# Two layer boundaries by halves of 128 tokens: a transformer forward pass on one Trainium2 core

## The chip, the cores and the metric

One NeuronCore of a Trainium2 chip. The metric is device microseconds of one execution on that core. The kernel is written engine by engine, with its semaphores set by hand: TensorE (PE in the profile) multiplies, VectorE (DVE) and ScalarE (ACT) do the elementwise work, GpSimd (POOL) helps, and SyncE (SP) issues the weight loads.

## The reference, cut to what matters

256 tokens with 2048 features go through two layers of the first block (gated attention of three kinds, then an output matrix and a LayerNorm), then through a second block. All is fp32. What the change touches:

```python
def hybrid_layer(x, mem, w_in, b_forget, w_mem_kv, w_out, ln_gain, ln_bias):
    h = jnp.einsum('bsd,dn->bsn', x, w_in)
    ...
    y = jnp.concatenate([y_fox, y_dsa, y_mem], axis=-1)
    y = jnp.einsum('bsn,nd->bsd', y, w_out)
    return layer_norm(ALPHA * x + y, ln_gain, ln_bias)
```

The LayerNorm is over the 2048 features of one token: rows do not depend on each other, but each needs the whole row of `y @ w_out`. What follows at both boundaries is a product with the normalised rows: layer 1's `w_in` after layer 0, the second block's `w_in` after layer 1.

## The kernel before, in words

**Blocks and the ring.** Every weight matrix is read in blocks of 128x1024 elements (512 KB). `plan` (line 94) lists the blocks in the order in which they are used; a chunk is the set of blocks that sum into one pair of accumulators `acc`, one accumulator bank for each half of 128 tokens (`s` = 0, 1). SP loads a block into a ring of four (`raw`, `RING` = 4). ScalarE rounds it to `high` (`round_block`, line 858), and VectorE forms what is left, `low = raw - high` (`low_part`, line 475). In some stretches, listed in `pool_blocks` (line 462), GpSimd does this instead: every second block from 40 to 133 of a layer and blocks 18 to 83 of the second block. The activations have a high and a low part as well (`xh`, `xl` for the features, `yh`, `yl` for the attention's output). TensorE forms high x high, high x low and low x high (`weight_block`, line 617). The high part of block g may be written only when TensorE has used block g - 4 (`block_used`), and `raw` only when its low part is formed.

**Chunks of w_out.** `COLS` (line 76) cuts the 2048 columns in three chunks of 512 and two of 256. In a chunk of 512 a block holds two row tiles of 512 columns, in one of 256 four row tiles of 256. A wide block is 2 row tiles x 2 token halves x 3 = 12 products of 512 columns; a narrow one 24 of 256. Both chunks of 256 together are the last eight blocks of a layer.

**The order of the work.** Each engine has its own program. Within a layer (162 blocks) VectorE and ScalarE keep ahead of TensorE through `slots` (line 400), and do side work between blocks. At the end of a layer `last_sides` (line 411) closes the list. Behind it, at the boundary:
- VectorE (lines 1465 to 1499) adds the residual of the last chunk when its last block is done (`add_residual`, line 1358), takes the statistics in pieces of 256 columns (line 1364), aggregates them per row (line 1470) and forms the variance.
- ScalarE takes the root (line 956); VectorE forms scale and shift of the rows in five small steps (lines 1233 to 1236, 1475).
- ScalarE normalises `x` in units of 256 columns, for both halves of the tokens (`normalise`, line 1044).
- TensorE, which has meanwhile run 36 filler products (`spin`, line 757, whose results nobody reads), transposes a unit into one of two banks `tb` (four 128x128 transposes, line 587).
- VectorE applies gain and bias out of the bank (`affine`, line 1478, products at line 1488), ScalarE rounds (`affine_high`, line 1051), VectorE forms the low part (line 1497).
- TensorE takes up the first block of the next product as soon as unit 0 is there. Block u needs unit u, since a block covers 256 features; the remaining six units are transposed between the blocks.

The order in time is what is written: an instruction that waits holds all behind it on its engine. The low parts of the first three blocks behind the boundary are formed by VectorE before the wait for the last product (`last_sides` with `LEAD - 1`; the third one behind it in the loop), and ScalarE rounds the first three in its `last_sides`.

**GpSimd** loads the rows of gain and bias at the boundary, when the last w_out block is used (lines 1734 and 1735); they are first needed by `residual` (line 1337), at block 18 of layer 1, or at block 3 of the second block, some 30 us after the boundary.

## Time and profile before

| what | value |
| --- | --- |
| median of 3 runs | 2205.16 us (2201.83 to 2205.2) |
| the profiled execution | 2201.67 us |
| its span, first to last instruction | 2199.9 us |
| mean granted clock of TensorE | 0.996 of full speed |

The profile describes one execution. Times in it are microseconds from its first instruction. A duration of an instruction includes its way through the engine, so that two in a row overlap by some 0.1 us in it. A row of the instructions in order of time ends, in brackets, with the idle time before it and what ended that. "issue" is time in which the engine waited for nothing that the profile shows. L662 is line 662 of the kernel.

### The profile page before, as it was taken

To read this page: it belongs to the slowest core of one execution; us is meant where nothing else is said; L and a number is where in the kernel's file an instruction comes from. 1 tells how busy PE (TensorE), PEld (TensorE's weight loads), DVE (VectorE), ACT (ScalarE), POOL (GpSimd) and SP (SyncE) were. 2 spreads that over 40 slices of the span, in tenths; PEclk is the share of its full clock that TensorE was granted. 3 is DMA by queue.
4 is the path that set the end of the run, shared out by engine and by line. 5 is a ranking of instruction groups with operands and counts; after the bars stand their busy time and mean duration, and the time that the engine had idled before them with its cause. 6 is when DMAs were issued, how large, how long until landed. Compare 5 with 4: busy or idle time off the path is not lost.

```text
span 2199.9 us, 29501 instructions
## 1 busy us (share of the span) xinstructions
PE 2157.8 (98%) x11798; PEld 1864.2 (85%) x11798; DVE 1278.4 (58%) x1851; ACT 1101.3 (50%) x1525; POOL 401.4 (18%) x176
## 2 busy tenths in 40 slices
PE   8999999999999999999999999999999999999997
PEld 7888888888988888888888888788888888888886
DVE  5544448765566337855577666665555555555555
ACT  4444554554354554555455455646535534544543
POOL 0000333431000334332006876000000000000000
PEclk9999999999999999999999999999999999999998
DMA  8666555655666555565656655545666666666663
GB/s 279 194 182 186 157 149 158 177 163 173 191 177 190 163 153 153 169 176 163 188 168 200 191 174 161 191 145 170 192 192 192 190 192 192 189 192 193 190 192 126
DMA packets 324313, 394.66 MB, mean 179 GB/s; under 512 B 20257, under 2 KB 252321, under 8 KB 323409
## 3 DMA queue, kind: packets, MB, share of 16 engines
q1 hardware_dynamic: 322528, 383.20, 57.9%
q0 software_dynamic: 1648, 9.58, 1.2%
q8 instruction: 94, 1.54, 0.3%
q14 instruction: 43, 0.34, 0.0%
HBM read 390.63 MB, written 2.10 MB: 179 GB/s over the span
## 4 chain that ended last, share of the span: by engine, by line
PE 90%; DVE 4%; ACT 3%; issue 2%; DMA 1%; SPq 0%; DVEq 0%; ACTq 0%
PE acc L645 32%; PE acc L660 16%; PE acc L662 12%; PE acc L647 12%; PE acc L648 12%; ACT high L863 1%; PE tb L708 1%; PE tb L587 1%; ACT sc L895 1%; PE obank L730 1%; DVE low L477 1%; PE sbank L754 1%; ACT sc L906 0%; PE sbank L698 0%; DVE yf L1225 0%
## 5 line engine op out<-in xcount | busy, mean ns | idle before, releaser
L863 ACT ACTIVATE high<-raw 128x1024 fp32r<-128x1024 f32 (+1 forms) x729 | 764.4, 1051 | 789.8 <-PE acc L660 197.9
L477 DVE TENSOR_TENSOR low<-raw,high 128x1024 fp32r<-128x1024 f32 (+1 forms) x569 | 710.6, 1250 | 632.6 <-ACT high L863 629.5
L645 PE MATMUL acc<-xhl,high 128*128 128x512 f32 x3200 | 778.7, 393 | 4.1 <-ACT cb L1152 2.2
L645 PEld LDWEIGHTS acc<-xhl,high 128*128 128x128 f32 x3200 | 585.8, 189 | 117.2 <-issue 2.8
L477 POOL TENSOR_TENSOR low<-raw,high 128x1024 fp32r<-128x1024 f32 x160 | 393.8, 2465 | 744.2 <-ACT high L863 744.0
L660 PE MATMUL acc<-xhl,low 128*128 128x256 f32 x3200 | 432.3, 285 | 2.7 <-DVE low L477 1.4
L660 PEld LDWEIGHTS acc<-xhl,low 128*128 128x128 f32 x3200 | 416.1, 191 | 20.9 <-DVE xhl L1643 1.7
L647 PE MATMUL acc<-high,yhl 128*128 128x512 f32 (+1 forms) x1044 | 383.8, 374 | 1.4 <-DVE work L1517 1.4
L648 PE MATMUL acc<-high,yhl 128*128 128x512 f32 (+1 forms) x1044 | 382.0, 372 | 0.0
L662 PE MATMUL acc<-low,yhl 128*128 128x512 f32 (+1 forms) x1044 | 242.9, 373 | 0.5 <-DVE yhl L1619 0.2
L647 PEld LDWEIGHTS acc<-high,yhl 128*128 128x128 f32 x1044 | 196.7, 188 | 36.1 <-DVE work L1517 1.8
L648 PEld LDWEIGHTS acc<-high,yhl 128*128 128x128 f32 x1044 | 196.7, 188 | 34.0
L662 PEld LDWEIGHTS acc<-low,yhl 128*128 128x128 f32 x1044 | 184.8, 188 | 35.7 <-DVE yhl L1619 1.1
L647 PE MATMUL acc<-high,xhl 128*128 128x512 f32 (+1 forms) x320 | 108.1, 353 | 1.0 <-issue 1.0
L1200 DVE TENSOR_TENSOR acc<-acc,cross 128x512 f32<-128x512 f32 x104 | 72.3, 695 | 61.8 <-ACT cross L883 61.6
L648 PE MATMUL acc<-high,xhl 128*128 128x512 f32 (+1 forms) x320 | 106.5, 349 | 0.0
L1553 DVE SCALAR_TENSOR_TENSOR tb<-work,params,tb 128x256 f32<-128x256 f32 x232 | 93.6, 481 | 0.0
L895 ACT ACTIVATE sc<-sc,small 128x128 f32<-128x128 f32 x64 | 28.6, 448 | 107.5 <-DVE small L1276 107.5
L662 PE MATMUL acc<-low,xhl 128*128 128x512 f32 (+1 forms) x320 | 69.8, 354 | 0.0
L647 PEld LDWEIGHTS acc<-high,xhl 128*128 128x128 f32 x320 | 61.0, 190 | 10.0 <-issue 2.2
L648 PEld LDWEIGHTS acc<-high,xhl 128*128 128x128 f32 x320 | 61.0, 191 | 7.5
L883 ACT ACTIVATE cross<-acc 128x512 f32<-128x512 f32 x104 | 60.4, 580 | 0.0
(199 smaller groups left out, 1268.2 us busy)
## 6 DMA issues: line engine op xcount, KB each, us to landing
raw<-in_w_in SPq DMA_DIRECT2D x336, 512.0 KB, 3.7
raw<-in_w_ff SPq DMA_DIRECT2D x256, 512.0 KB, 4.4
raw<-in_w_out SPq DMA_DIRECT2D x91, 512.0 KB, 4.5
raw<-in_w_mem_kv SPq DMA_DIRECT2D x32, 512.0 KB, 4.7
raw<-in_w_out SPq DMA_DIRECT2D x10, 256.0 KB, 2.7
x_nat<-in_mem SPq DMA_DIRECT2D x4, 512.0 KB, 7.6
x_nat<-in_x POOLq DMA_DIRECT2D x4, 512.0 KB, 5.7
yf<-in_ln_gain POOLq DMA_DIRECT2D x2, 1024.0 KB, 5.2
```

The lines of the kernel that those rows point to most:

```text
L477: eng.tensor_tensor(part(low, g), part(raw, g), part(high, g).bitcast(F32), ALU.subtract).then_inc(ready, 1)
L587: ins = pe.transpose(t[:, dt * S + s * P:dt * S + s * P + P], src[:, s, first + dt * P:first + dt * P + P], ident)
L645: ins = pe.matmul(acc[:, 2 * (c.acc % 2) + s, :], wh[:, t, at], vhl, start=first, stop=last)
L647: pe.matmul(outs[s], vh[:, at], wh[:, t, :], start=first, stop=False)
L648: ins = pe.matmul(outs[s], vl[:, at], wh[:, t, :], start=False, stop=last)
L660: ins = pe.matmul(acc[:, 2 * (c.acc % 2) + s, S:2 * S], wl[:, t, at], vh, start=False, stop=last)
L662: ins = pe.matmul(outs[s], vh[:, at], wl[:, t, :], start=False, stop=last)
L863: act.activation(part(high, g), part(raw, g), ACT.Copy).then_inc(high_ready, 1)
L883: act.activation(cross, crosses(c), ACT.Copy).then_inc(cross_ready, 1)
L895: ins = act.activation(sc[:, j % 2, s, 0:n], src, ACT.Exp, bias=nmx[:, r:r + 1], accum_out=rs[:, r:r + 1])
L1200: dve.tensor_tensor(accs(c), accs(c), cross, ALU.add).then_inc(folded, 1)
L1553: ins = dve.scalar_tensor_tensor(out=cv[:, ct, :] if tap == TAPS - 1 else sums_at, in0=src, scalar=w, in1=sums_at, op0=ALU.mult, op1=ALU.add)
```

## The change

The output matrix is cut in four chunks of 512 columns (`FCOLS`) instead of five. The last four blocks of w_out (`out`) and the first four behind the boundary (`into`) are passed twice, first for tokens 0 to 127, then for tokens 128 to 255; all four stay in the ring meanwhile. `weight_block` takes the halves as `rows`; `block_used` rises at the second pass, and the new semaphore `rows_half` when the last of `out` has been passed for the first half. TensorE's order is written out in `edge`, and the filler is gone. Residual, statistics, variance, root, scale and the first four units of normalising, transposing, gain and bias, rounding and low part are done per half. The statistics are taken over 512 columns at once, everywhere. The low parts of the first three blocks of `into` go to GpSimd, ahead of its loads of the rows; ScalarE rounds these blocks only behind the first root. The counters of the semaphores follow. The filler before the feed-forward stage stays.

```diff
-        for n, (col, width) in enumerate(COLS):
+        for n, (col, width) in enumerate(FCOLS):
...
-        def norms(phase, u):
-            return 5 * phase + (u + 1 if u < 2 else 2 + u // 2)
+        def norms(phase, u, s=0):
+            if phase < DEPTH:
+                return 8 * phase + (3 * s + min(u, 2) + 1 if u < 4 else 7 + (u - 4) // 2)
+            return 8 * DEPTH + (u + 1 if u < 2 else 2 + u // 2)
+        def tiles_in(phase, u, s=0):
+            return 12 * phase + (4 * s + u + 1 if u < 4 else 8 + u - 3)
+        edges = [(by[("o", l, NF - 1)].blocks[-4:], by[("fv", l + 1, 0) if l + 1 < DEPTH else ("v2", 0)].blocks[:4])
+                 for l in range(DEPTH)]
...
-        pool_blocks = [[LAYER0 + LAYER_SLOTS * l + b for b in range(40, 134) if b % 2] for l in range(DEPTH)]
+        pool_blocks = [[LAYER0 + LAYER_SLOTS * l + b for b in range(40, 134) if b % 2] + edges[l][1][:3]
+                       for l in range(DEPTH)]
...
-            def weight_block(g):
+            def weight_block(g, rows=(0, 1)):
...
-                tiles = [(t, c.kt0 + c.nk * i + t, s) for t in range(c.nk) for s in range(len(outs))]
+                tiles = [(t, c.kt0 + c.nk * i + t, s) for t in range(c.nk) for s in rows[:len(outs)]]
...
-                ins.then_inc(block_used, 1)
+                if 1 in rows:
+                    ins.then_inc(block_used, 1)
+                elif g == c.blocks[-1]:
+                    ins.then_inc(rows_half, 1)
...
+            def half_transposes(l, s, u):
+                pe.wait_ge(norm_ready, norms(l, u, s))
+                t = t_begin(("nT", l, u, s))
+                for dt in range(2):
+                    ins = pe.transpose(t[:, dt * S + s * P:dt * S + s * P + P],
+                                       x[:, s, 256 * u + dt * P:256 * u + dt * P + P], ident)
+                t_end(ins, ("nT", l, u, s))
+            def full_transposes(l, u):
+                pe.wait_ge(norm_ready, norms(l, u))
+                transpose_unit(("nT", l, u), x, 256 * u)
+            def edge(l):
+                out, into = edges[l]
+                for g in out:
+                    weight_block(g, (0,))
+                for g in out[:3]:
+                    weight_block(g, (1,))
+                half_transposes(l, 0, 0)
+                weight_block(out[3], (1,))
+                half_transposes(l, 0, 1)
+                half_transposes(l, 0, 2)
+                weight_block(into[0], (0,))
+                half_transposes(l, 0, 3)
+                weight_block(into[1], (0,))
+                weight_block(into[2], (0,))
+                half_transposes(l, 1, 0)
+                weight_block(into[3], (0,))
+                half_transposes(l, 1, 1)
+                half_transposes(l, 1, 2)
+                weight_block(into[0], (1,))
+                half_transposes(l, 1, 3)
+                weight_block(into[1], (1,))
+                full_transposes(l, 4)
+                weight_block(into[2], (1,))
+                full_transposes(l, 5)
+                weight_block(into[3], (1,))
+                for u in range(4, 8):
+                    if u < 6:
+                        full_transposes(l, u + 2)
+                    weight_block(into[3] + u - 3)
...
-                spin(job_no(l, "dsa", HS - 1), 36)
-                for u in range(2):
-                    pe.wait_ge(norm_ready, norms(l, u))
-                    transpose_unit(("nT", l, u), x, 256 * u)
+                edge(l)
...
-                last_sides(round_block, layer_side, g0, LAYER_SLOTS)
+                last_sides(round_block, layer_side, g0, LAYER_SLOTS, 0)
                 nxt = g0 + LAYER_SLOTS
-                root(l + 1)
+                root_half(0)
+                round_block(nxt)
+                act.wait_ge(nmr_ready, 2 * l + 1)
+                normalise(0, 1, (0,))
+                normalise(1, 1, (0,))
+                round_block(nxt + 1)
+                affine_high(0, 0)
+                normalise(2, 2, (0,))
+                affine_high(1, 0)
+                round_block(nxt + 2)
+                affine_high(2, 0)
+                root_half(1)
+                affine_high(3, 0)
                 round_block(nxt + 3)
-                act.wait_ge(nmr_ready, l + 1)
-                normalise(0)
-                normalise(1)
-                normalise(2, 2)
-                for u in range(8):
-                    affine_high(8 * l + u)
-                    if u in (0, 2):
-                        normalise(u + 4, 2)
-                    if u >= 2:
-                        round_block(nxt + 2 + u)
+                act.wait_ge(nmr_ready, 2 * l + 2)
+                normalise(0, 1, (1,))
+                normalise(1, 1, (1,))
+                affine_high(0, 1)
+                normalise(2, 2, (1,))
+                affine_high(1, 1)
+                normalise(4, 2, (0, 1))
+                affine_high(2, 1)
+                affine_high(3, 1)
+                round_block(nxt + 4)
+                normalise(6, 2, (0, 1))
+                round_block(nxt + 5)
+                for u in range(4, 8):
+                    affine_high(u)
+                    round_block(nxt + 2 + u)
...
+                def row_stats(n, s):
+                    last[0] = step(dve.bn_stats(stats[:, s, n, :], x[:, s, CW * n:CW * n + CW]))
...
+                def last_residual(s, l=l):
+                    n = NF - 1
+                    c = by[("o", l, n)]
+                    at = x[:, s, CW * n:CW * n + CW]
+                    if s:
+                        acc_done(c)
+                    else:
+                        dve.wait_ge(rows_half, l + 1)
+                    ins = dve.scalar_tensor_tensor(out=at, in0=at, scalar=ALPHA, in1=accs(c)[:, s, :], op0=ALU.mult,
+                                                   op1=ALU.add)
+                    if s:
+                        ins.then_inc(sum_ready, 1)
+                        dve.wait_ge(sum_ready, sums("o", l, n))
+                    else:
+                        link(ins)
+                def row_var(s):
+                    dve.wait_ge(dve_done, last[0])
+                    link(dve.bn_aggr(mv[:, s, :], stats[:, s, :, :].rearrange("p c k -> p (c k)")))
+                    dve.tensor_scalar(var[:, s:s + 1], mv[:, s, 1:2], LN_EPS, None, ALU.add).then_inc(var_ready, 1)
+                def row_scale(s, l=l):
+                    at = slice(s, s + 1)
+                    dve.wait_ge(std_ready, 2 * l + s + 1)
+                    link(newton(var[:, at], std[:, at], rstd[:, at], nt[:, at]))
+                    dve.scalar_tensor_tensor(out=nmr[:, at], in0=mv[:, s, 0:1], scalar=-1.0, in1=rstd[:, at], op0=ALU.mult,
+                                             op1=ALU.mult).then_inc(nmr_ready, 1)
...
-                last_sides(low_block, layer_side, g0, LAYER_SLOTS, LEAD - 1)
-                nxt = g0 + LAYER_SLOTS
-                add_residual(NC - 1)
-                dve.wait_ge(dve_done, last[0])
-                for s in range(ST):
-                    step(dve.bn_aggr(mv[:, s, :], stats[:, s, :, :].rearrange("p c k -> p (c k)")))
-                dve.wait_ge(dve_done, n_done[0])
-                dve.tensor_scalar(var, mv[:, :, 1], LN_EPS, None, ALU.add).then_inc(var_ready, 1)
-                dve.wait_ge(std_ready, l + 1)
-                link(newton(var, std, rstd, nt))
-                dve.scalar_tensor_tensor(out=nmr, in0=mv[:, :, 0], scalar=-1.0, in1=rstd, op0=ALU.mult,
-                                         op1=ALU.mult).then_inc(nmr_ready, 1)
-                def affine(n):
...
+                def affine(u, s=0, l=l):
+                    t = t_wait(dve, ("nT", l, u, s) if u < 4 else ("nT", l, u))
...
+                    for dt in range(2):
+                        kt = 2 * u + dt
+                        at = slice(dt * S + s * P, dt * S + s * P + P) if u < 4 else slice(dt * S, dt * S + S)
+                        ins = dve.tensor_scalar(cb[:, u % 4, at], t[:, at], g[:, kt:kt + 1], b_[:, kt:kt + 1],
+                                                ALU.mult, ALU.add)
+                    ins.then_inc(aff_ready, 1)
+                def affine_low(u, s=0, l=l):
+                    at = slice(s * P, s * P + P) if u < 4 else slice(0, S)
+                    dve.wait_ge(hi_ready, 16 + tiles_in(l, u, s))
+                    dve.tensor_tensor(xl[:, 2 * u:2 * u + 2, at], pair(cb[:, u % 4, :])[:, :, at],
+                                      xh[:, 2 * u:2 * u + 2, at].bitcast(F32), ALU.subtract).then_inc(xt_ready, 1)
+                last_sides(low_block, layer_side, g0, LAYER_SLOTS, 0)
+                nxt = g0 + LAYER_SLOTS
+                last_residual(0)
+                row_stats(NF - 1, 0)
+                row_var(0)
+                row_scale(0)
+                affine(0, 0)
+                affine_low(0, 0)
+                affine(1, 0)
+                last_residual(1)
+                affine_low(1, 0)
+                affine(2, 0)
+                row_stats(NF - 1, 1)
+                affine_low(2, 0)
+                affine(3, 0)
+                row_var(1)
+                affine_low(3, 0)
+                row_scale(1)
+                low_block(nxt + 3)
+                affine(0, 1)
+                affine(1, 1)
+                affine_low(0, 1)
+                affine(2, 1)
+                affine_low(1, 1)
+                affine(3, 1)
+                affine_low(2, 1)
+                affine_low(3, 1)
+                low_block(nxt + 4)
+                affine(4)
+                low_block(nxt + 5)
+                for u in range(4, 8):
                     if u < 7:
-                        affine(8 * l + u + 1)
-                    dve.wait_ge(hi_ready, 16 + 8 * l + u + 1)
-                    dve.tensor_tensor(xl[:, 2 * u:2 * u + 2, :], pair(cb[:, u % 4, :]),
-                                      xh[:, 2 * u:2 * u + 2, :].bitcast(F32), ALU.subtract).then_inc(xt_ready, 1)
+                        affine(u + 1)
+                    affine_low(u)
                     low_block(nxt + 2 + u)
```

## Rows read from the trace of the kernel before

**Rows 1.** The page, busy time: us (share of the span) xinstructions.

```profile
PE 2157.8 (98%) x11798; PEld 1864.2 (85%) x11798; DVE 1278.4 (58%) x1851; ACT 1101.3 (50%) x1525; POOL 401.4 (18%) x176
```

**Rows 2.** The chain of waits, 592 to 640 us: start, us, what.

```profile
594.79 1.92 PE acc L662 x16
...
616.91 0.44 PE tb L587 x4
...
634.73 1.81 PE acc L662 x8
```

**Rows 3.** Instructions of TensorE in order of time, both boundaries: start, us, line, shapes.

```profile
604.23 4.48 PE L761 MATMUL sbank<-xhl 128*128 128x256 f32 x36
...
612.83 0.76 PE L647 MATMUL acc<-high,xhl 128*128 128x512 f32 x1 [0.32 <-issue]
...
638.20 0.28 PE L641 MATMUL sbank<-xhl,high 128*86 128x256 f32 x1
...
1114.17 4.48 PE L761 MATMUL sbank<-xhl 128*128 128x256 f32 x36
...
1122.77 0.47 PE L647 MATMUL acc<-high,xhl 128*128 128x512 f32 x1 [0.64 <-issue]
...
1147.04 1.98 PE L645 MATMUL acc<-xhl,high 128*128 128x512 f32 x8
```

**Rows 4.** The chain of waits at the first boundary: start, us, what.

```profile
604.43 0.70 DVE x_nat L1358
605.15 0.76 DVE small L1364 x2
605.94 0.61 DVE small L1470 x2
...
606.78 0.21 ACT small L956
...
608.00 3.50 ACT x_nat L1048 x6
```

**Rows 5.** Groups by line and shape: xcount, busy us, mean ns, idle before.

```profile
L863 ACT ACTIVATE high<-raw 128x1024 fp32r<-128x1024 f32 x715 | 755.1, 1058 | 774.2 <-PE acc L660 197.9 <-PE acc L645 188.5 <-PE acc L662 184.7
...
L477 POOL TENSOR_TENSOR low<-raw,high 128x1024 fp32r<-128x1024 f32 x160 | 393.8, 2465 | 744.2 <-ACT high L863 744.0
...
L926 ACT ACTIVATE yhl<-y 128x256 fp32r<-128x256 f32 x32 | 13.2, 413 | 0.4 <-DVE y L1295 0.4
...
L1364 DVE BATCH_NORM_STATS2 small<-x_nat 128x6 f32<-128x256 f32 x32 | 11.4, 415 | 0.3
...
L1497 DVE TENSOR_TENSOR xhl<-cb,xhl 128x512 fp32r<-128x512 f32 x16 | 11.0, 684 | 0.4 <-ACT xhl L1054 0.4
...
L1048 ACT ACTIVATE x_nat<-x_nat,small 128x512 f32<-128x512 f32 x12 | 9.0, 801 | 0.0
...
L1488 DVE TENSOR_SCALAR cb<-tb,params 128x256 f32<-128x256 f32 x16 | 8.0, 540 | 4.7 <-PE tb L587 4.7
...
L1254 DVE SCALAR_TENSOR_TENSOR yf<-tb,small,consts 128x128 f32<-128x128 f32 x12 | 4.2, 352 | 34.8 <-PE tb L689 34.8
```

**Rows 6.** One line of VectorE: xcount, min/median/max ns, first and last start us.

```profile
L1301 DVE TENSOR_TENSOR yhl<-y,yhl x32: 399/420/2605, 240.2 to 1044.3; 128x256 fp32r<-128x256 f32 x32
```

**Rows 7.** Instructions of GpSimd and VectorE in order of time, 486 to 492 and 871 to 877 us.

```profile
487.21 2.39 POOL L477 TENSOR_TENSOR low<-raw,high 128x1024 fp32r<-128x1024 f32 x1 [4.50 <-ACT high L863]
487.29 2.58 DVE L1301 TENSOR_TENSOR yhl<-y,yhl 128x256 fp32r<-128x256 f32 x1
...
871.47 2.41 POOL L477 TENSOR_TENSOR low<-raw,high 128x1024 fp32r<-128x1024 f32 x1 [2.15 <-ACT high L863]
872.65 0.69 DVE L1222 TENSOR_TENSOR cb<-acc,consts 128x512 f32<-128x512 f32 x1
```

**Rows 8.** Busy time by stretch: us, PE, PEld, DVE, ACT, POOL busy (x), granted clock, DMA share, GB/s.

```profile
610.00:615.00 5.00, 3.80 (x13) 2.81 (x14) 4.78 (x9) 4.13 (x8) 0.00 (x0) 0.67 0.32 124
...
1120.00:1125.00 5.00, 3.54 (x18) 2.72 (x19) 4.78 (x9) 4.13 (x8) 0.00 (x0) 1.00 0.36 125
```

101 lines of the change are left out of this document (46 added, 55 removed).

## The prediction

> **What bounds the kernel now.** I read the page first, then the order of time on TensorE around each layer boundary, then the chain of waits there. TensorE is busy for 98% of the span [rows 1], so only what TensorE computes, or where it computes nothing, can move the time. A product with 512 columns takes 0.227 us at the full clock, one with 256 takes 0.12 [rows 2]. A block of the narrow kind (24 products of 256) therefore takes 2.88 us, a wide one (12 of 512) 2.72, and a unit of four transposes 0.44 [rows 2].
>
> At the boundary between the layers the last product of w_out ends at 604.23, the next layer's first starts at 612.83, and its eighth block is done at 638.20; at the second boundary these are 1114.17, 1122.77 and 1147.04 [rows 3]. Between, TensorE runs filler products and three transpose units. Count each boundary from the first of the last eight w_out blocks (8 x 2.88 = 23.04 before 604.23) to the end of the eighth block behind it: 638.20 - 581.19 = **57.0 us**, and 1147.04 - 1091.13 = **55.9 us**. The work in it is 23.04 + 8 x 2.72 + 8 x 0.44 = 48.3, so 8.7 and 7.6 us are stalls, 16.3 together. The chain shows what fills them: the residual (0.70), the statistics (0.76 and 0.61), root and scale, and six normalising steps in a row (3.50) [rows 4]. The filler costs nothing now and its removal gives nothing.
>
> The first boundary is 1.1 us longer than the second, with the same steps: there the granted clock is 0.67 in the 5 us around the return of the products, at the second 1.00 [rows 8]. TensorE had run filler and then only transposes before it fell.
>
> **The change, part by part.**
>
> *Wide last blocks.* The eight w_out blocks of columns 1536 to 2047 become wide: 8 x 0.16 = 1.3 us less per boundary, on TensorE's path and hidden by nothing. The residual in mid-way falls away beside other work. I take **-2.6 us** for both; this is the surest term.
>
> *The new order.* The last four w_out blocks pass for rows 0 to 127, then for rows 128 to 255, and the norm of the first half runs under the second pass. Half a block is 6 x 0.227 = 1.36 us. The number of products and of transposes stays the same, so the work from the first of these four blocks to the eighth behind is 12 x 2.72 + 8 x 0.44 = 36.2 us. The question is how much stall is left. VectorE must do more: each affine unit of the first four is cut in two pieces. I take for the new shapes:
> - affine on 128 columns out of PSUM: 0.41 us, between 0.35 (a row of that shape, another operation) and 0.54 (256 columns) [rows 5]. Issued behind one another each costs 0.09 less. A unit thus costs 2 x 0.64 = 1.3 instead of 0.9.
> - statistics over 512 columns: 0.67, from 0.41 for 256 [rows 5] plus 256 elements more, which cost 0.26 on VectorE between 420 ns [rows 6] and 684 [rows 5]. Bounds 0.41 and 0.82.
> - ScalarE's rounding of half a unit: 0.41 [rows 5], bounds 0.35 and 0.63; normalising 0.80 for 512 columns [rows 5] and 0.5 in a row for 256, as now (six steps of both kinds take 3.50, [rows 4]). The low parts of the activations by halves: 0.42 [rows 6], bounds 0.35 and 0.68.
> - The low parts of the next three weight blocks move to GpSimd: 2.40 us each where nothing holds it up (mean 2.47, [rows 5]), instead of 1.2 on VectorE.
>
> That last move has a price that the list of durations hides. While GpSimd forms a low part (487.21, 2.39 us), a VectorE subtraction of 128x256 with both inputs in SBUF takes 2.58 us instead of the median 0.42 [rows 6]; it ends just after GpSimd does. One with an input in PSUM runs at its usual 0.69 in the middle of such a step [rows 7]. So the affine steps and the residual (PSUM) run on, but the low parts of the activations (both inputs in SBUF) wait for GpSimd. The Trainium skill (SBUF — State Buffer, SBUF: two separate sides) says that a VectorE instruction with two SBUF inputs and a GpSimd one hold a shared port pair exclusively, and whoever starts first blocks the other for the whole instruction. By that rule the sum is the one below; without it, it would be the first rival's.
>
> Now laid out by hand, each engine in its written order, 0.03 us from an engine to the next (0.1 to a product), time 0 at the first of the last four blocks:
> - 5.44: first half passed. Residual, statistics, aggregate, variance to 7.55; root 7.58 and five small steps to 8.73, 1.2 in all as now (606.78 to 608.00, [rows 4]); ScalarE, having rounded weight block 0 from 7.69 to 8.74 (1.06, [rows 5]), normalises units 0 and 1 by 9.84. TensorE is still in the second pass: the transposes of unit 0 start at 9.52 with **no stall**, where 8.6 us lie between the products now. This is what the change wins.
> - GpSimd's low part of block 0 runs 8.82 to 11.22, just when VectorE wants its first subtraction, at 11.15. VectorE gets in at 11.22; GpSimd's next runs 11.56 to 13.96, the third 14.30 to 16.70. VectorE's second and third subtractions wait for the ends of these, at 13.96 and 16.70.
> - Stalls of TensorE: **0.5** (unit 2 normalised), **0.8** (low part of unit 1), **1.4** (of unit 2).
> - VectorE reaches the second half's variance only at 18.0 and its scale at 20.0, since it also has the third and fourth affine units of the first half. TensorE has finished block 2 at 18.6 and waits for the second half's first transposes until 20.7: **2.1**. Then 0.3 for the low part of block 3, which stands behind the scale on VectorE, 0.2 and **0.9** for the first subtraction of half two.
> - From there no stall until block 4: VectorE has the low part of block 4, affine unit 4, the low part of block 5 and affine unit 5 (1.2 + 0.9 + 1.2 + 0.9, and half a microsecond of waits, from 28.1) in front of unit 4's subtraction, done at 33.2; TensorE is ready at 31.2: **2.1**. After it the old rhythm holds.
>
> Sum of stalls 8.4 per boundary, 44.6 us to the end of the eighth block. With the four wide blocks ahead (10.9): 55.5 for each boundary. Before: 57.0 and 55.9. **Sum: 2 x 55.5 - 112.9 = -1.9 us**; in words, -2.6 by wide blocks, and stalls of 16.9 for 16.3, cut small but not shortened. The falling clock of the first boundary is in the 57.0 and taken as gone.
>
> *Edits at nothing:* the LayerNorm row loads leave GpSimd's queue only behind its third low part (16.7), some 6 us behind the last w_out block instead of at once, and are needed 30 us after the boundary; that slack is their cover, and without it VectorE's later residual would wait. SP's queue has each weight load behind the low part four blocks earlier: block 4's load can start after 11.2 and is wanted at 27, some 16 us for a load, while the steady rhythm has one land every 2.7. Counters and names cost nothing.
>
> The profiled execution took 2201.67 us (span 2199.9); the median of the three runs is 2205.16, 3.5 above it. -1.9 from the median gives **2203.3**. A measurement of this kernel can tell about 0.2%, 4.4 us, from no change.
>
> **The rivals.**
> - *The port does not bind*, because GpSimd's steps miss VectorE's. The same layout without it has stalls of 0.6, 0.2, 1.6, 0.3, 0.2, 0.9 and 2.1, so 42.2 instead of 44.6: 53.1 per boundary, -6.7 us: **2198.5**. For it: VectorE works much on PSUM. Against: the steps that ended with GpSimd's [rows 7], and the two want the port in the same 0.1 us.
> - *GpSimd wins the first race.* VectorE asks at 11.15 and GpSimd is free at 11.22; 0.1 us more in the rounding of the half unit, and GpSimd's second low part goes first, until 13.6. Then block 0 itself waits 1.9 and the third block 2.0: 46.6, or 57.5 per boundary, +2.1: **2207.3**. If the half affine costs 0.54, or the rounding 0.63, the same branch comes out, with some 47.5 at the most, +3.9.
> - *The clock falls in the new gaps*, the slower one. Twice per boundary TensorE has only transposes and waits for over 2.5 us (18.6 to 21.3, and 30.8 to 33.3). A fall costs 1.1 (57.0 against 55.9) to 1.7 us (a granted clock of 0.67 over 5 us, [rows 8]). Four falls: -1.9 + 4.4 to 6.8, up to **2210.1**. It decides from four falls at 1.6 each on. For it: the clock fell once in two such gaps. Against: those gaps held 4 us without a full stretch of products, the new ones less. The Trainium skill (TensorE: Matmul & The Clock Gate, HAM oscillation) says that short groups of products between waits throttle again and again; that speaks against this change, and by it the time is this rival's.
> - *The change does not act*, since the second pass still waits for all rows: the semaphore for the first half is raised by the last of the four first-half passes, so no; in the rest.
>
> **How the numbers follow.** Forecast 0.37 (no change), port free 0.22 (faster), GpSimd first 0.24 (no change), clock 0.11 (slower), rest 0.06, half to each side. So faster 0.25, within 0.2% 0.61, slower 0.14. The range takes in the first rival with half a microsecond below it, and the second with its dearest shapes (+3.9, 2209.1): 2198.0 to 2209.3.
>
> **What would show it.** In the profile after: no filler, and transposes starting at once behind the third second-half block (right or wrong for the overlap); VectorE subtractions of 128x256 with 1.2 us or more beside GpSimd steps (the port); TensorE idle before the second half's first transposes and before the fifth block, 2 us each; granted clock 1.00 at both boundaries. TensorE idle below 6 us per boundary would show the layout too dear, one product group at half clock the third rival.

## The result, and the profile after

The changed kernel takes 2207.82 us (median of 13 runs, 2206.4 to 2210.43) where the kernel before takes 2203.35 (13 runs, 2200.14 to 2206.61): a ratio of 1.0021, with a 95% interval of 1.0013 to 1.0030. The forecast was 2203.3, a shade below the kernel before; the time came out 4.5 us above it, inside the range that was given and on its slow side. The forecast had started from 2205.16, the median of three runs, which lies 1.8 above the median of thirteen: as a change, -1.9 was forecast and +4.5 came, which is a miss of 6.4. The profiled execution has a span of 2204.6, against 2199.9.

Busy time on the page of the changed kernel; TensorE's is 7.6 us less than before [rows 1], though two fillers of 4.48 us are gone [rows 3], so what it computes takes no less time than it did, and the longer span is more idle time:

```profile
PE 2150.2 (98%) x11534; PEld 1845.8 (84%) x11534; DVE 1283.1 (58%) x1865; ACT 1101.5 (50%) x1535; POOL 415.7 (19%) x182
```

Instructions of TensorE in order of time at the first boundary and, behind the second line of dots, at the second: start, us, line, shapes, and in brackets the idle time ahead and what ended it. The last row of each group is the first product behind the eighth block. They answer to [rows 3].

```profile
600.83 0.38 PE L775 MATMUL tb<-consts,x_nat 128*128 128x128 f32 x2
...
603.19 0.44 PE L775 MATMUL tb<-consts,x_nat 128*128 128x128 f32 x2 [0.38 <-ACT x_nat L1098]
605.20 0.47 PE L657 MATMUL acc<-high,xhl 128*128 128x512 f32 x1 [1.57 <-issue]
...
609.93 0.50 PE L657 MATMUL acc<-high,xhl 128*128 128x512 f32 x1 [1.43 <-DVE xhl L1586]
...
613.42 0.44 PE L775 MATMUL tb<-consts,x_nat 128*128 128x128 f32 x2 [1.85 <-ACT x_nat L1098]
...
617.07 0.47 PE L657 MATMUL acc<-high,xhl 128*128 128x512 f32 x1 [0.79 <-issue]
...
626.25 0.50 PE L657 MATMUL acc<-high,xhl 128*128 128x512 f32 x1 [1.86 <-DVE xhl L1586]
...
639.34 0.28 PE L651 MATMUL sbank<-xhl,high 128*86 128x256 f32 x1
...
1112.72 0.38 PE L775 MATMUL tb<-consts,x_nat 128*128 128x128 f32 x2
...
1151.21 1.07 PE L655 MATMUL acc<-xhl,high 128*128 128x512 f32 x4
```

The filler is gone, the first transposes of the half (600.83) stand among the products of w_out, and the products that take the new operand begin at 605.20, 7.6 us earlier than before (612.83). So the overlap that the change is written for is there. But TensorE is stopped seven times behind the first half transposes, 8.0 us in all (six of the seven are shown; the seventh is 0.15 at 614.02). From the first half transposes to the end of the eighth block it takes 38.5 us at each boundary; the first of the last eight w_out blocks starts 20.4 us ahead of them, in this kernel and in every one below that has its TensorE order. That makes **58.9 us for both boundaries**, where the kernel before has 57.0 and 55.9: +1.9 and +3.0, together 4.9, and the spans differ by 4.7. The rest of the kernel is the same within 0.8 us.

Two causes are to be seen. The first is in GpSimd's and VectorE's instructions in order of time, first and second boundary. The row in the second place shows the second of the two low parts of the row ahead of it by itself:

```profile
600.10 4.72 POOL L487 TENSOR_TENSOR low<-raw,high 128x1024 fp32r<-128x1024 f32 x2 [83.88 <-ACT high L913]
602.47 2.35 POOL L487 TENSOR_TENSOR low<-raw,high 128x1024 fp32r<-128x1024 f32 x1
602.47 2.63 DVE L1586 TENSOR_TENSOR xhl<-cb,xhl 128x256 fp32r<-128x256 f32 x1 [0.49 <-ACT xhl L1108]
...
607.96 1.92 DVE L1586 TENSOR_TENSOR xhl<-cb,xhl 128x256 fp32r<-128x256 f32 x1
...
1112.00 4.72 POOL L487 TENSOR_TENSOR low<-raw,high 128x1024 fp32r<-128x1024 f32 x2 [83.88 <-ACT high L913]
1114.37 2.63 DVE L1586 TENSOR_TENSOR xhl<-cb,xhl 128x256 fp32r<-128x256 f32 x1 [0.49 <-ACT xhl L1108]
```

GpSimd runs its first two low parts one behind the other. The rows of the second low part and of VectorE's first subtraction both start at 602.47, a tie to the hundredth of a microsecond. The low part takes its usual 2.35 and the subtraction 2.63 instead of 0.42: it ends 0.28 behind the second low part (605.10 and 604.82), so GpSimd had the port. Block 0 waits for it (605.20). The row calls that wait "issue"; who is late is read from VectorE's row.

The second cause is the clock. Busy time by stretch (the columns are those of [rows 8]; the third figure from the right is the granted clock), and one product of that stretch:

```profile
625.00:630.00 5.00, 3.75 (x10) 3.00 (x11) 4.97 (x8) 2.21 (x3) 0.00 (x0) 0.71 0.83 155
...
1140.00:1145.00 5.00, 5.00 (x20) 3.94 (x19) 3.63 (x7) 2.32 (x3) 0.00 (x0) 0.75 0.69 210
```

```profile
627.46 0.63 PE L657 MATMUL acc<-high,xhl 128*128 128x512 f32 x1
```

A product of 512 columns takes 0.23 us from the start of one to that of the next; from 627.05 to 629.16 the starts are 0.42 apart, the 1.2 GHz level in place of 2.4. Ahead of it TensorE had waited 1.86 us before the fifth block; the clock was still high for the first 0.8 us of products behind that wait (626.25 to 627.05). This happens once per boundary, behind the same wait, where before it happened at the first boundary only.

### The profile page after: what moved, and what is told of

Same layout as the page of the kernel before. It is cut to its first block, busy times and chain, and to the rows that moved or that the text cites. A ratio compares the mean times of both kernels' runs of the same rounds, so it can differ in the third digit from the quotient of the medians.

```text
span 2204.6 us, 29019 instructions
## 1 busy us (share of the span) xinstructions
PE 2150.2 (98%) x11534; PEld 1845.8 (84%) x11534; DVE 1283.1 (58%) x1865; ACT 1101.5 (50%) x1535; POOL 415.7 (19%) x182
## 3 DMA queue, kind: packets, MB, share of 16 engines
q1 hardware_dynamic: 318432, 383.20, 57.8%
## 4 chain that ended last, share of the span: by engine, by line
PE 89%; DVE 6%; ACT 3%; issue 2%; DMA 1%; SPq 0%; DVEq 0%; ACTq 0%
PE acc L655 32%; PE acc L670 16%; PE acc L672 12%; PE acc L657 12%; PE acc L658 12%; ACT high L913 1%; PE tb L721 1%; DVE low L487 1%; ACT sc L945 1%; PE obank L743 1%; DVE xhl L1586 1%; PE sbank L767 1%; ACT sc L956 0%; PE tb L597 0%; PE sbank L711 0%
## 5 line engine op out<-in xcount | busy, mean ns | idle before, releaser
L487 DVE TENSOR_TENSOR low<-raw,high 128x1024 fp32r<-128x1024 f32 (+2 forms) x563 | 703.1, 1250 | 630.3 <-ACT high L913 627.3
L487 POOL TENSOR_TENSOR low<-raw,high 128x1024 fp32r<-128x1024 f32 x166 | 408.2, 2463 | 910.2 <-ACT high L913 910.0
L657 PE MATMUL acc<-high,yhl 128*128 128x512 f32 (+1 forms) x980 | 377.6, 387 | 1.4 <-DVE work L1641 1.4
L658 PE MATMUL acc<-high,yhl 128*128 128x512 f32 (+1 forms) x980 | 375.8, 385 | 0.0
L657 PEld LDWEIGHTS acc<-high,yhl 128*128 128x128 f32 x980 | 184.2, 188 | 38.5 <-DVE work L1641 1.8
L658 PEld LDWEIGHTS acc<-high,yhl 128*128 128x128 f32 x980 | 184.1, 188 | 36.4
L672 PEld LDWEIGHTS acc<-low,xhl 128*128 128x128 f32 x320 | 52.7, 193 | 9.5 <-issue 2.1
```

The costliest lines, as they stand in the source:

```text
L487: eng.tensor_tensor(part(low, g), part(raw, g), part(high, g).bitcast(F32), ALU.subtract).then_inc(ready, 1)
L657: pe.matmul(outs[s], vh[:, at], wh[:, t, :], start=first, stop=False)
L658: ins = pe.matmul(outs[s], vl[:, at], wh[:, t, :], start=False, stop=last)
L672: ins = pe.matmul(outs[s], vh[:, at], wl[:, t, :], start=False, stop=last)
```

## Experiments

"Boundaries" are counted as above, from the first of the last eight w_out blocks to the end of the eighth block behind, in the profiled execution. "Ratio" is to runs of the kernel before on the same chip, with its 95% interval; the median of before there stands beside it.

| kernel | median us (n) | before | ratio | boundaries us |
|---|---|---|---|---|
| changed | 2207.82 (13) | 2203.35 | 1.0021 [1.0013, 1.0030] | 58.9, 58.9 |
| e1 wide blocks alone | 2204.18 (11) | 2202.31 | 1.0007 [0.9998, 1.0016] | 56.8, 57.9 |
| e2 GpSimd's low parts short | 2201.39 (11) | 2202.31 | 0.9992 [0.9983, 1.0001] | 56.5, 55.2 |
| e3 GpSimd waits | 2201.95 (11) | 2202.31 | 0.9995 [0.9986, 1.0004] | 57.8, 57.2 |
| e4 fillers | 2203.69 (11) | 2202.31 | 1.0002 [0.9994, 1.0011] | 55.4, 55.4 |
| e6 e3 and e4 | 2201.38 (11) | 2201.94 | 0.9997 [0.9988, 1.0006] | 55.6, 55.7 |
| e11 VectorE late, fillers | 2205.25 (11) | 2203.34 | 1.0007 [0.9998, 1.0016] | 57.3, 57.3 |
| e12 VectorE late | 2208.32 (11) | 2203.34 | 1.0023 [1.0014, 1.0032] | 58.9, 58.9 |
| e9 two lines exchanged | 2205.11 (11) | 2202.69 | 1.0010 [1.0001, 1.0020] | 56.1, 56.1 |
| e5 reordered | 2197.65 (11) | 2201.94 | 0.9977 [0.9968, 0.9986] | 52.6, 52.6 |
| e7 reordered, two low parts | 2197.85 (8) | 2201.94 | 0.9976 [0.9966, 0.9987] | 52.8, 52.8 |
| e8 reordered, GpSimd waits | 2194.61 (5) | 2201.94 | 0.9964 [0.9952, 0.9977] | 50.9, 50.9 |
| e10 reordered, exchanged | 2196.06 (5) | 2202.69 | 0.9961 [0.9949, 0.9974] | 51.4, 51.3 |

### e1: the wide blocks alone

The kernel before, with w_out in four chunks of 512 columns.

```
-        for n, (col, width) in enumerate(COLS):
+        for n, (col, width) in enumerate(FCOLS):
             c = chunk(("o", l, n), a["w_out"][l], col, width=width)
...
-                add_residual(NC - 1)
+                add_residual(NF - 1)
```

> The kernel before with the output matrix cut in four chunks of 512 columns and nothing else of the change. By the sum of the prediction this alone is worth 8 x 0.16 us per boundary: 2.6 us less than the kernel before, a ratio of 0.9988, with the boundary itself (filler, three units of transposes, first product 8.6 us after the last) as it was. If instead the narrow blocks cost nothing on TensorE's path, the ratio is 1.000. If the slowing of the changed kernel came from the wide cut, this kernel is slower than before.

No gain: 1.0007, with an interval that leaves out the 2.6 us (0.9988). In order of time, TensorE, VectorE, and TensorE again:

```profile
602.59 4.47 PE L761 MATMUL sbank<-xhl 128*128 128x256 f32 x36
...
602.79 1.22 DVE L1358 SCALAR_TENSOR_TENSOR x_nat<-x_nat,acc 128x1024 f32<-128x1024 f32 x1 [3.06 <-PE acc L648]
604.05 1.41 DVE L1364 BATCH_NORM_STATS2 small<-x_nat 128x6 f32<-128x256 f32 x4
...
612.38 0.77 PE L647 MATMUL acc<-high,xhl 128*128 128x512 f32 x1 [0.18 <-issue]
```

The products end at 602.59 instead of 604.23, 1.6 us earlier: 1.3 by the eight wide blocks, and 0.4 because the first of them starts earlier (580.83 for 581.19). But the last chunk is now 512 columns for the norm's chain too: the residual takes 1.22 for 0.70 and the statistics 1.41 for 0.76 [rows 4]. The first product is 0.45 us earlier, at 612.38. The first boundary, with one fall of the clock before and here, is 0.2 us shorter (56.8 for 57.0). The second is 2.0 longer (57.9 for 55.9): there the clock falls here (0.50 at 1120 to 1125) and did not before. In front of a serial chain, a wider last chunk moves work from TensorE to the chain.

### e2: GpSimd's part of the port taken away

```
                 for g in pool_blocks[l]:
+                    if g in edges[l][1]:
+                        pool.wait_ge(high_ready, g + 1)
+                        n = slice(0, 32)
+                        pool.tensor_tensor(part(low, g)[:, :, n], part(raw, g)[:, :, n], ...)
+                        continue
                     low_part(pool, g, low_pool)
```

It leaves out 480 of 512 columns of three low parts per boundary.

> The changed kernel, with GpSimd's three low parts at each boundary formed for 32 of 512 columns only (the rest of these low parts is left out), so that GpSimd holds the shared port for a moment instead of 2.4 us each. All waits and orders stay. Port theory: no VectorE subtraction of 128x256 takes over 0.5 us, the stalls before blocks 0 and 2 of the new product go, and the eight blocks of w_out to the eighth behind the boundary take 53.1 to 53.3 us instead of 58.9, up to 9 us less in all than the changed kernel, ratio to the kernel before 0.997. Rival (the halves themselves cost it, VectorE's doubled instructions): under 2 us less than the changed kernel.

GpSimd now takes 0.32 us a block, and no subtraction of VectorE is above 0.43. TensorE's first product with the new operand is at 603.87, right behind the transposes:

```profile
600.59 0.32 POOL L1858 TENSOR_TENSOR low<-raw,high 128x64 fp32r<-128x64 f32 x1 [83.84 <-ACT high L913]
...
603.87 0.48 PE L657 MATMUL acc<-high,xhl 128*128 128x512 f32 x1
```

Counted from the first half transposes, that product comes after 2.56 us instead of 4.37, and the waits of 1.57 before block 0 and 1.43 before block 2 are gone. The ratio falls by 0.0029, 6.4 us. The rival, that the doubled instructions of the halves are what costs, had allowed less than 2. The clock falls in three stretches still, two at the first boundary and one at the second; less 1.6 for each, the 56.5 and 55.2 would be 53.3 and 53.6, near the 53.1 laid out for a port that does not bind.

### e3: the tie decided by a wait

```
                 for g in pool_blocks[l]:
+                    if g == edges[l][1][1]:
+                        pool.wait_ge(xt_ready, 16 + tiles_in(l, 0, 0))
                     low_part(pool, g, low_pool)
```

> The changed kernel with one wait more: GpSimd starts its second low part only after VectorE's first subtraction of the boundary, which it beat by some 0.03 us. Port theory with the race: the first product behind the boundary starts 1.6 us sooner, 2.0 us less per boundary, 4 us less than the changed kernel in all, about level with the kernel before. If the order of the two does not matter: the time of the changed kernel.

VectorE, GpSimd and VectorE in order of time:

```profile
602.92 0.43 DVE L1586 TENSOR_TENSOR xhl<-cb,xhl 128x256 fp32r<-128x256 f32 x1 [0.50 <-ACT xhl L1108]
...
603.42 4.92 POOL L487 TENSOR_TENSOR low<-raw,high 128x1024 fp32r<-128x1024 f32 x2 [0.47 <-DVE xhl L1586]
...
604.65 1.44 DVE L1586 TENSOR_TENSOR xhl<-cb,xhl 128x256 fp32r<-128x256 f32 x1
...
607.26 1.36 DVE L1586 TENSOR_TENSOR xhl<-cb,xhl 128x256 fp32r<-128x256 f32 x1
```

This is the forecast's order: the first subtraction runs free, the second and third end with GpSimd's second and third. The ratio falls by 0.0026, 5.7 us where 4 were expected, for one wait on a queue that has time. The clock still falls at both boundaries of this execution (0.50 at 615 to 620, 0.66 at 1135 to 1140), which is why they read 57.8 and 57.2. But it is one of the slower ones: its mean granted clock is 0.994, and seven of the eleven have 0.996 or 0.997. The waits of the layout are there as well (0.45, 0.87, 1.83, and 1.49 to 1.87 before the fifth block).

### e4: fillers in the two long gaps

Fourteen filler products before the second half's first transposes and fourteen before the fifth block.

```
                 weight_block(into[2], (0,))
+                spin(job_no(l, "dsa", HS - 1), 14)
                 half_transposes(l, 1, 0)
...
+                    if u == 4:
+                        spin(job_no(l, "dsa", HS - 1), 14)
                     weight_block(into[3] + u - 3)
```

> The changed kernel with 14 filler products (1.7 us, results read by nobody) in each of the two longest gaps of each boundary, before the transposes of the second half's first unit and before the fifth block. Clock theory: the granted clock stays at 1.00 at both boundaries and each is 1.2 to 1.4 us shorter, 2.5 us in all. Rival: the clock's fall is no part of the difference, or comes from the waits before these gaps: no change, or up to 0.5 us longer where a filler product stands before one that could start.

The clock stays at 1.00 through both boundaries. But the profiled execution shows something else too:

```profile
600.36 7.57 POOL L487 TENSOR_TENSOR low<-raw,high 128x1024 fp32r<-128x1024 f32 x3 [83.85 <-ACT high L916]
...
602.72 0.42 DVE L1589 TENSOR_TENSOR xhl<-cb,xhl 128x256 fp32r<-128x256 f32 x1 [0.51 <-ACT xhl L1111]
```

VectorE won the port here, with nothing changed ahead of it. GpSimd's second low part, by itself, starts at 602.72 as well and takes 2.67 instead of 2.35. At the second boundary its row starts at 1111.01 and VectorE's at 1111.02, and VectorE won there too. The two ask in the same hundredth of a microsecond, and it has gone either way; which of them gets the port can't be told from the starts. The single times lie in two groups, four at 2200.2 to 2200.8 and seven at 2203.1 to 2205.3, with none between. The mean granted clock is 0.996 or 0.997 in the first group and 0.995 or 0.996 in the second, so the clock can be a part of what parts them, but not all: at 0.996 there are 2200.21 and 2203.91. One run thus changed two things, and e6, e11 and e12 take them apart.

### e6, e11, e12: the port and the clock, one at a time

e6 has the edits of e3 and e4. e12 makes VectorE late, by three aggregates ahead of its first subtraction, and e11 has that and the fillers:

```
                 affine(0, 0)
+                for _ in range(3):
+                    link(dve.bn_aggr(mv[:, 0, :], stats[:, 0, :, :].rearrange("p c k -> p (c k)")))
                 affine_low(0, 0)
```

> The changed kernel with both repairs: GpSimd's second rounding remainder waits for VectorE's first 256-column subtraction, and 14 filler matmuls stand before the second half's first transposes and before the fifth block. Theory (the loss is the lost race at the port, 1.8 to 2.0 us a boundary, plus granted-clock falls, 1.3 us a boundary, and nothing else): both boundaries measure 55.4 us from the first of the last eight w_out blocks, no granted clock under 1 within either boundary, times in one narrow group (not the two groups, 2200.2 to 2200.8 and 2203.1 to 2205.3, that the fillers alone gave), median near 2200.5, ratio near 0.999. Rival (the two groups of the fillers alone were clock, not the race): two groups again, median near 2203. Rival (the fillers cost what they give): median as with the wait alone, ratio 0.9995, boundaries above 57.

> The changed kernel with the two groups of 14 filler matmuls, and VectorE held up by three aggregates (0.3 us each, their result the one that stands there) ahead of its first subtraction, so that GpSimd's second remainder always starts first. Theory (in the run with fillers alone the executions at 2200.2 to 2200.8 won the tie at the port, and those at 2203.1 to 2205.3 lost it): one group now, at 2203 to 2205.5, both boundaries 57.2 to 57.5 us, no granted clock under 1 within them, ratio 1.0008 to 1.0014. Rival (the two groups were clock): still two groups, or a median below 2202.

> The changed kernel with the three aggregates alone. Theory: the changed kernel always loses the tie, so the aggregates lie inside a wait that is there anyway and cost nothing: the changed kernel's ratio, 1.0015 to 1.0027, boundaries 58.9 us with one fall of the granted clock in each. What it is above the kernel with fillers as well is the price of the falls in a kernel that loses the tie: 3 to 3.5 us. Rival (the falls cost what they fill, as the pair with the wait suggests, 0.6 us): the two are within 1 us.

e6 has one group (2198.8 to 2202.2), no clock under 1 at a boundary, and boundaries of 55.6 and 55.7: the layout of the forecast (55.5) with both losses off. Its median is 0.9 above what I expected, and the fillers gain 0.6 at most over e3.

e11 has lost the tie at both boundaries. GpSimd and VectorE:

```profile
599.93 4.72 POOL L487 TENSOR_TENSOR low<-raw,high 128x1024 fp32r<-128x1024 f32 x2 [83.87 <-ACT high L916]
...
602.60 2.33 DVE L1589 TENSOR_TENSOR xhl<-cb,xhl 128x256 fp32r<-128x256 f32 x1
```

The boundaries are 57.3 each, 1.7 above e6, and the median is 3.9 above e6's (2.5, if each is first held against its own runs of before). There is one group, at 2202.6 to 2206.6, wider than expected. In e11 the clock fell once, at 605 to 610 (0.66), and the boundary was no longer than the other: the slow products took up the wait of 1.43 us ahead of block 2, which the other boundary has (TensorE is busy for 4.97 of these 5 us, for 3.37 in the changed kernel).

e12 is the changed kernel again (1.0023 for 1.0021, the same 58.9 twice), so three extra instructions inside a wait cost nothing. Against e11 it is 3.1 us slower: the price of the clock's falls in a kernel that loses the tie. In this execution the clock fell in four places of the two boundaries, two more than expected, also behind the wait for block 0. The two more cost nothing, since the next wait took them up (the boundaries are 58.9 as in the changed kernel):

```profile
605.00:610.00 5.00, 4.68 (x14) 3.46 (x14) 4.97 (x10) 1.78 (x3) 2.66 (x2) 0.66 0.50 154
625.00:630.00 5.00, 3.64 (x10) 2.82 (x11) 5.00 (x8) 2.22 (x4) 0.00 (x0) 0.69 0.80 149
```

So the 4.5 us of the result are: -0.6 for the layout by itself (e6 against before), +2.5 for the port (e11 against e6), +3.1 for the clock (e12 against e11), 5.0 in all for e12 and 4.5 for the changed kernel. Each of these differences of medians is known to 2 to 3 us only, and the -0.6 can't be told from nothing. The boundaries of the profiled executions say the same more sharply: 112.9 before, 111.2 in e6 (-1.7), 114.6 in e11 (+3.4), 117.8 in e12 (+3.2), together +4.9. With the tie won, the fillers bring 0.6 or nothing (e6 against e3); with the tie lost they bring 3.1. That the longer waits of a lost tie make the clock fall more often is an argument, not shown; e9, below, speaks against the tie as the only reason.

### e9: the tie decided by order, without a wait

```
-                round_block(nxt + 1)
                 affine_high(0, 0)
+                round_block(nxt + 1)
                 normalise(2, 2, (0,))
```

> The changed kernel with two neighbouring lines of ScalarE's order exchanged: the first operand's half is rounded ahead of the second weight block. GpSimd's second remainder has then nothing to start on until 0.4 us or more after VectorE's first subtraction has been asked for, with no wait added. Theory (a tie at the port, 0.04 us apart, decides 1.8 to 2.0 us a boundary): no VectorE subtraction of 2.63 us, the first product 2.4 to 2.6 us behind the first half transposes (4.37 in the changed kernel), a median of 2201 to 2202.5, as with the wait (ratio 0.9990 to 1.0002). Rival (GpSimd's long operations cost the subtraction a wait wherever they lie): the 2.63 us moves to the second or third subtraction, and the median stays above 2205. Both: boundaries of 55.4 to 57.8 us, by how often the granted clock falls.

The tie is won at both boundaries, and no subtraction takes more than 1.63. But only half of the 4.5 us comes back (1.0010), the median is 2.6 us above what I expected at the most, and the first product comes 3.50 us behind the first half transposes, not 2.4 to 2.6. The expectation had looked at GpSimd only. ScalarE:

```profile
603.44 0.42 ACT L1108 ACTIVATE xhl<-cb 128x256 fp32r<-128x256 f32 x1 [0.82 <-DVE cb L1578]
603.76 1.04 ACT L913 ACTIVATE high<-raw 128x1024 fp32r<-128x1024 f32 x1
604.71 0.80 ACT L1098 ACTIVATE x_nat<-x_nat,small 128x512 f32<-128x512 f32 x1
```

and TensorE:

```profile
605.56 0.44 PE L775 MATMUL tb<-consts,x_nat 128*128 128x128 f32 x2 [1.32 <-ACT x_nat L1098]
```

ScalarE now waits 0.82 us for VectorE ahead of the exchanged pair, and the 1.04 us of the weight block fall between that wait and normalising units 2 and 3. In the changed kernel they had filled the wait. The transposes of unit 2 wait 1.32 instead of 0.38.

That costs 0.5 us a boundary (56.1, with no fall of the clock in them, for e6's 55.6), 1 of the 2.6. The rest is not in this execution, which is the fastest of the eleven (2202.71, mean granted clock 0.997): eight of the others have 0.993 or 0.994 and take 2204.4 to 2208.4. It is put down to the clock, though none of those eight was profiled. In the profiled one the clock stays up behind the very wait that it falls behind in the changed kernel:

```profile
626.43 0.50 PE L657 MATMUL acc<-high,xhl 128*128 128x512 f32 x1 [1.87 <-DVE xhl L1586]
```

```profile
625.00:630.00 5.00, 3.57 (x18) 2.98 (x19) 5.00 (x8) 2.74 (x5) 0.00 (x0) 1.00 0.79 135
```

So a wait of 1.9 us does not by itself decide whether the clock falls.

### e5, e7, e8, e10: the orders of ScalarE and VectorE written anew

TensorE's order and all the work are those of the changed kernel. The heart of e5, on VectorE:

```
                 affine_low(0, 0)
-                affine(1, 0)
                 last_residual(1)
+                affine(1, 0)
+                row_stats(NF - 1, 1)
                 affine_low(1, 0)
                 affine(2, 0)
-                row_stats(NF - 1, 1)
-                affine_low(2, 0)
                 affine(3, 0)
                 row_var(1)
-                affine_low(3, 0)
+                affine_low(2, 0)
                 row_scale(1)
+                affine_low(3, 0)
...
                 low_block(nxt + 5)
-                for u in range(4, 8):
-                    if u < 7:
-                        affine(u + 1)
-                    affine_low(u)
-                    low_block(nxt + 2 + u)
+                affine_low(4)
+                affine(5)
...
```

Thus the second half's mean and variance come ahead of the first half's last subtractions, and unit 4's subtraction ahead of unit 5's affine. On ScalarE weight block 3 goes ahead of the second half's root, and that half's first four units are all normalised ahead of its first rounding. e7 also gives block 0's low part back to VectorE and orders some roundings and subtractions differently again; e8 is e5 with the wait of e3; e10 is e5 with the exchange of e9.

> The changed kernel with TensorE's order as it is and ScalarE's and VectorE's orders at the edge written so that the operand comes first and the fourth to last roundings later; GpSimd keeps its three remainders. Theory (the stalls of the change are places in two hand-written orders): the stalls before the second half's first transposes and before the fifth block fall from 1.8 us each to under 0.5, a boundary from 58.9 to about 51 if VectorE wins the race at the port, about 53 if it does not; together 11 us under the kernel before at best, median 2192 to 2197. Rival (the fifth block waits for its rounding, which waits for a ring slot, whatever the order): the stall of 1.9 us before the fifth block stays and the median is above 2199.

> As the reordered one, but the first block's remainder on VectorE ahead of the first affine, and GpSimd keeps the second and third alone. Theory (the race needs two long GpSimd operations back to back): no VectorE subtraction of 256 columns above 1.5 us, boundary about 51 us, median 2191 to 2195, at least as good as the reordered one. Rival (the 0.7 us of the remainder on VectorE stands on the path before the first product): the first product of the block comes 0.7 us later, and the median is no better than the reordered one's.

> The reordered kernel with GpSimd's second remainder behind VectorE's first subtraction. Theory: if the reordered kernel loses the race, this is 1.5 to 2 us a boundary below it; if it wins there, the two are within 0.5 us of each other. Rival (GpSimd's third remainder comes too late for the third block when all three start later): a wait on low before the third block of over 0.5 us, and the median above the reordered one's.

> The reordered kernel with the same exchange (the second weight block's rounding behind the first operand half's) in place of the wait. Theory: as the reordered kernel with the wait, within 1 us: median 2194 to 2195.5, ratio 0.996 to 0.997, boundaries of 50.9 us each, and 2 us of it given back at the twelfth block behind the second boundary (waits of 1.3 on ScalarE's rounding and 1.9 on VectorE's remainder, where the kernel before waits 1.45). Rival (the second block's rounding is on the path once it comes 0.4 us later): a wait on low of 0.4 us or more before the second block, median above 2196.

e5 and e7 lose time at the port and gain all the same. e5's median is 0.65 above the most that I expected. In e5 the waits of 1.85 and 1.86 are gone. Its first subtraction, and e7's low part of block 0 and first two subtractions:

```profile
602.77 2.63 DVE L1591 TENSOR_TENSOR xhl<-cb,xhl 128x256 fp32r<-128x256 f32 x1 [0.50 <-ACT xhl L1108]
```

```profile
600.87 1.23 DVE L487 TENSOR_TENSOR low<-raw,high 128x1024 fp32r<-128x1024 f32 x1
...
604.29 3.42 DVE L1591 TENSOR_TENSOR xhl<-cb,xhl 128x256 fp32r<-128x256 f32 x2
```

e7's expectation fell: with two low parts on GpSimd in a row the port is lost as with three, only a block later, and with 1.23 us more on VectorE the transposes of unit 2 wait 1.98 us, where in e5 they wait 0.39. e8 has all of it. The waits of TensorE at its first boundary:

```profile
603.87 0.44 PE L775 MATMUL tb<-consts,x_nat 128*128 128x128 f32 x2 [0.39 <-ACT x_nat L1098]
606.38 0.74 PE L672 MATMUL acc<-low,xhl 128*128 128x512 f32 x2 [0.46 <-DVE xhl L1591]
608.90 0.50 PE L657 MATMUL acc<-high,xhl 128*128 128x512 f32 x1 [0.86 <-DVE xhl L1591]
611.31 0.71 PE L672 MATMUL acc<-low,xhl 128*128 128x512 f32 x2 [0.49 <-DVE low L487]
```

2.2 us of waits where the changed kernel has 8.0, boundaries of 50.9, and no clock under 1 in either. **e8 beats both kernels**: 2194.61, 0.9964 [0.9952, 0.9977] of the kernel before. e10 gets there without the wait (0.9961 [0.9949, 0.9974]); the two can't be told apart. Its boundaries are 0.5 longer than e8's and than expected, by the same 1.32 us before unit 2's transposes as in e9, and its median is 0.6 above the most expected; a wait for the second block's low part, the rival's sign, does not come.

The boundaries of e8 are 11.1 us shorter than before, its span only 7.1. Where 2 of the missing 4 went, TensorE and ScalarE show behind the second boundary:

```profile
1142.77 2.11 PE L655 MATMUL acc<-xhl,high 128*128 128x512 f32 x8 [1.28 <-ACT high L913]
1147.75 1.22 PE L670 MATMUL acc<-xhl,low 128*128 128x256 f32 x8 [1.92 <-DVE low L487]
```

```profile
1137.77 0.63 ACT L1015 ACTIVATE pt<-x_nat 128x512 f32<-128x512 f32 x1 [5.20 <-DVE x_nat L1422]
```

ScalarE has the squares of the residual ahead of the next rounding in its order, and stands for 5.2 us until VectorE has added the rows; TensorE, now early, waits 1.28 and 1.92 where, before the change and with it, it waited 1.4 for the second alone. Other orders there were not tried. Most of the rest goes at 1495 to 1500, where the clock falls in e8 (0.66) and does not in the profiled execution of before.

## Why the prediction was wrong

- **The overlap** was right: first half transposes without a stall behind the third second-half block, filler gone, each new shape within 0.03 us of the value taken (affine 0.73 a pair, statistics 0.69 for 0.67, half rounding 0.40 to 0.42 for 0.41).
- **The layout by hand** was right in its total: 55.5 laid out, 55.4 to 55.7 measured in e4 and e6. It was less right inside: the stalls are 6 us rather than 8.4 (5.9 and 6.3 in e3, which has no fillers in them), and the work some 2 us more than 47.1. The first product behind a wait takes 0.47 to 0.50 instead of 0.39.
- **The first step that failed** is the order at the port: "VectorE wants its first subtraction, at 11.15" and "gets in at 11.22", ahead of GpSimd's second low part. The sizes were right: counted from the same zero (591.30), both rows start at 11.17. But a sum of a dozen estimated durations cannot set two engines 0.07 us apart. They came within 0.01 of each other, and GpSimd got the port at both boundaries of the profiled execution; e12, made to lose, has the changed kernel's time. The rival "GpSimd wins the first race" named it, its price (57.5 a boundary) is what e11 shows (57.3), and its chance of 0.24 was far too low for a step that nothing decides.
- **The second step that failed**, and no smaller a one, is the clock: it was put at nothing in the new gaps, and "taken as gone" from the first boundary. It falls at both, behind the wait before the fifth block, +1.6 a boundary between 57.3 and 58.9, as the price of one fall (1.1 to 1.7) had it. The argument against it (the new gaps are shorter than the old ones) did not hold: a wait of 1.86 us came ahead of it. That removing the filler "gives nothing" went too far as well: with 14 filler products in each of two gaps e11 is 3.1 us faster than e12. What decides whether it falls stays open, since e9 has the same wait and no fall. The Trainium skill (TensorE: Matmul & The Clock Gate, HAM oscillation) has a kernel whose groups of products, each shorter than the wait for a DMA behind it, throttle again and again. Here 7 us of work stand ahead of the wait of 1.86, and the clock falls behind it in the changed kernel and in e12 all the same; the forecast gave this a chance of 0.11.
- These two rivals were priced one by one, and what came is both. That 2207.82 lies near the port rival's 2207.3 is luck: its +2.1 stood on a start that was 1.8 too high, and the clock's +3.1 (e12 against e11) is not in it. The same 1.8 put the time inside the range: counted from 2203.35, the range would have ended at 2207.5.
- **"The surest term"**, -2.6 by wide blocks, is true on TensorE (the eight blocks take 21.8 instead of 23.0 in e1). Made alone, it is taken back by a residual and statistics of twice the width. In the changed kernel the halves hide these; its share there was not measured by itself.
- **The port** itself was right: subtractions beside GpSimd's low parts take up to 2.63 for 0.42 and end some 0.3 behind them, and affine steps out of PSUM beside them keep their 0.73. The Trainium skill (SBUF — State Buffer, SBUF: two separate sides) has whoever starts first block the other for the whole instruction, and the runs agree, in both directions: in e4, where VectorE's 0.42 came first, GpSimd's second low part takes 2.67 instead of 2.35.

## What to carry to other kernels

Where two engines want one port within a tenth of a microsecond of each other, treat the outcome as open, price both branches, and write the order into the kernel: one wait on the engine with time in hand gave back 5.7 us here, of which e11 and e12 put about half down to fewer falls of the clock. Look past the one wait in the profile before exchanging two lines, since work that fills a wait becomes a delay when it is moved behind it. When a serial stage is cut in halves, its gain goes to whichever engine's hand-written order still serves the old flow; the change alone cost 4.5 us, and only with the orders of ScalarE and VectorE rewritten and that wait (-12.6 us against the changed kernel) did it pay.

## What the runs showed of the hardware that I had not expected

- Two requests for the port in the same hundredth of a microsecond have gone either way: GpSimd got it at 602.47 in the changed kernel and at 602.77 in e5, VectorE at 602.72 in e4. That it also differs from one execution of a kernel to the next is inferred, not seen: e4's times fall in two groups some 3.8 us apart, its profiled execution won the tie at both boundaries, and the slower group lies where e11 does (1.8 and 1.9 above their own runs of before).
- A VectorE request that stands well before GpSimd's low part ends gets in ahead of GpSimd's next: in e7 VectorE asks at 604.29, 0.6 us before a low part ends, and has the port before the next low part, which then takes 2.57.
- TensorE's clock fell behind waits of 1.6 to 1.9 us (605 to 610 and 625 to 630 in e12), and not behind every such wait (none behind 1.87 in e9's profiled execution). The mean differs between executions of one kernel: e3's seven fastest times have a mean granted clock of 0.996 or 0.997 and its four slowest, some 1.7 us above, 0.993 or 0.994.
